# A hybrid decoder layer on one NeuronCore: other orders of the same steps on TensorE, ScalarE and VectorE

## What is computed

```
z  = rms_norm(h) @ w_in                         # 3328 columns: RWKV-7 inputs and q, k, v
h += concat(rwkv7_time_mix(z), moba(q, k, v)) @ w_mix_out
h += cross_attention(rms_norm(h), rms_norm(mem))  # 4 heads of 256: w_xq, w_xkv, w_xo
h += square(relu(rms_norm(h) @ w_ff1)) @ w_ff2    # 1024 -> 4096 -> 1024
out = rms_norm(h)
```

## Time and profile before

| | us |
|---|---|
| median of 3 runs | 488.88 |
| the profiled execution, its own time | 492.94 |
| its span in the trace | 491.0 |
| TensorE busy (matmuls) | 467.5 |
| VectorE busy | 331.4 |
| ScalarE busy | 238.4 |

### The profile page before, as it was taken

How to read it: one execution, slowest core, us unless ns; L and a number is a source line. 1 busy time by engine, 2 the same in 40 slices (tenths; PEclk the granted TensorE clock), 3 DMA queues, 4 the chain that set the end, 5 groups by cost and what they waited for, 6 DMA issues and landing times.

```text
span 491.0 us, 10602 instructions
## 1 busy us (share of the span) xinstructions
PE 467.5 (95%) x4518; PEld 422.9 (86%) x4518; DVE 331.4 (68%) x492; ACT 238.4 (49%) x384; POOL 35.6 (7%) x55
## 2 busy tenths in 40 slices
PE   4899999999899999989999999999999999999995
PEld 4899999989887889989999898887888888888883
DVE  3976998975156883946955569567656485756656
ACT  5788625245074433424644454555444443544444
POOL 8300000000000000015100024000000000000000
PEclk9997999999799999999999999999999999999999
DMA  7945254330233342255552236356575557466522
GB/s 251 298 160 174 87 172 131 118 101 10 81 110 90 121 137 87 87 172 171 167 178 85 87 94 206 130 166 192 167 246 156 195 166 238 159 245 191 157 82 85
DMA packets 61411, 73.07 MB, mean 149 GB/s; under 512 B 1315, under 2 KB 51573, under 8 KB 61365
## 3 DMA queue, kind: packets, MB, share of 16 engines
q1 hardware_dynamic: 61284, 72.14, 45.8%
q0 software_dynamic: 80, 0.26, 0.2%
HBM read 71.35 MB, written 1.05 MB: 147 GB/s over the span
## 4 chain that ended last, share of the span: by engine, by line
PE 74%; DVE 15%; ACT 4%; issue 3%; DMA 1%; SPq 1%; DVEq 0%; ACTq 0%
PE bank L522 8%; PE bank L536 8%; PE bank L538 8%; PE bank L537 8%; PE bank L554 6%; PE bank L556 6%; PE bank L555 6%; DVE w_lo L1271 5%; PE bank L520 5%; PE bank L744 2%; PE bank L489 2%; ACT w_hi L971 2%; PE bank L491 2%; PE bank L490 2%; PE bank L897 1%
## 5 line engine op out<-in xcount | busy, mean ns | idle before, releaser
L1271 DVE TENSOR_TENSOR w_lo<-raw,w_hi 128x1024 fp32r<-128x1024 f32 x130 | 159.9, 1240 | 66.9 <-ACT w_hi L971 66.6
L971 ACT ACTIVATE w_hi<-raw 128x1024 fp32r<-128x1024 f32 x130 | 136.0, 1056 | 107.1 <-PE bank L538 51.5
L536 PE MATMUL bank<-op,w_hi 128*128 128x256 f32 x416 | 123.0, 296 | 4.1 <-DVE w_lo L1271 2.3
L537 PE MATMUL bank<-op,w_hi 128*128 128x256 f32 x416 | 118.4, 285 | 0.0
L538 PE MATMUL bank<-op,w_lo 128*128 128x256 f32 x416 | 118.3, 284 | 0.0
L536 PEld LDWEIGHTS bank<-op,w_hi 128*128 128x128 f32 x416 | 80.5, 194 | 7.3 <-issue 4.8
L537 PEld LDWEIGHTS bank<-op,w_hi 128*128 128x128 f32 x416 | 80.6, 194 | 0.2
L538 PEld LDWEIGHTS bank<-op,w_lo 128*128 128x128 f32 x416 | 80.4, 193 | 0.0
L522 PE MATMUL bank<-op,w_hi 128*128 128x512 f32 x224 | 80.0, 396 | 0.0
L520 PE MATMUL bank<-op,w_lo 128*128 128x256 f32 x256 | 66.4, 280 | 0.1
L520 PEld LDWEIGHTS bank<-op,w_lo 128*128 128x128 f32 x256 | 48.3, 189 | 2.9 <-DVE op L1352 0.4
(11 more groups left out here) (254 smaller groups left out, 612.1 us busy)
## 6 DMA issues: line engine op xcount, KB each, us to landing
raw<-in_w_ff SPq DMA_DIRECT2D x32, 1024.0 KB, 5.4
raw<-in_w_in SPq DMA_DIRECT2D x12, 1024.0 KB, 5.3
raw<-in_w_xkv SPq DMA_DIRECT2D x8, 1024.0 KB, 5.5
raw<-in_w_mix_out SPq DMA_DIRECT2D x4, 1024.0 KB, 5.2
raw<-in_w_xq SPq DMA_DIRECT2D x4, 1024.0 KB, 5.1
raw<-in_w_xo SPq DMA_DIRECT2D x4, 1024.0 KB, 5.2
xval<-in_x SPq DMA_DIRECT2D x2, 512.0 KB, 4.8
raw<-in_w_in SPq DMA_DIRECT2D x2, 512.0 KB, 5.8
```

Source lines behind the costliest of these rows:

```text
L536: mm(dst, wh[:, k, :], op_hi[which][:, k, :], start=first, stop=False)
L537: mm(dst, wh[:, k, :], op_lo[which][:, k, :], start=False, stop=False)
L971: op(view(w_hi), r, ACT.Copy).then_inc(hi_done, 1)
L1271: tt(view(w_lo), r, view(w_hi).bitcast(f32), ALU.subtract).then_inc(lo_done, 1)
```

## The change

Three lists of steps are replaced by others with the same steps; no step's own code changes, but for one wait added to `shifted` on VectorE (for `dve_bonus`). The lists of TensorE, ScalarE and VectorE in short, with "..." for parts that are left out:

```diff
 TensorE
-load(0, 0); params(0); load(0, 1); load(0, 2); load(0, 3); dense(2); params(1); dense(3); spread(0)
-dense(3); lora(); dense(8); key_sums(); dense(1); key_spread(); dense(8); spread(1); dense(6)
-load(1, 0); load(1, 1); tokens(); dense(1); bonus(); dense(1); values_turn(); dense(1); mats(0)
-load(1, 2); dense(2); load(1, 3); mats(1); dense(4); right(0); right(1); dense(3); right(2)
-right(3); dense(2); solve(0); solve(1); solve(2); pair_scores(0); solve(3); carry(0); carry(1)
-carry(2); carry(3); dense(2); solved(0); solved(1); solved(2); solved(3); dense(3); outq(0, 0)
-outq(0, 1); outq(0, 2); dense(1); pair_turn(0, 0); outq(0, 3); outq(1, 0); outq(1, 1); dense(1)
-pair_turn(0, 1); outq(1, 2); outq(1, 3); dense(1); pair_values(0); dense(1); phi(0); pair_scores(1)
-phi(1); dense(2); psi(0, 0); psi(0, 1); psi(0, 2); psi(0, 3); psi(1, 0); dense(1); psi(1, 1)
-psi(1, 2); psi(1, 3); dense(2); pair_turn(1, 0); pair_turn(1, 1); state(1); pair_values(1); dense(1)
-pair_scores(2); dense(2); state(2); dense(2); pair_turn(2, 0); pair_turn(2, 1); state(3)
-pair_values(2); dense(1); pair_scores(3); dense(1); state(4); dense(1); state(5); dense(1)
-pair_turn(3, 0); dense(1); pair_turn(3, 1); state(6); dense(1); states_out(); pair_values(3)
-dense(1); center(); dense(3); deviation(); dense(2); normalize(); gate(); dense(24); rms(2)
-dense(5); scores(0); dense(4); scores(1); turn(0); ...
+load(0, 0); params(0); load(0, 1); load(0, 2); load(0, 3); dense(2); params(1); dense(2); spread(0)
+dense(6); lora(); dense(6); key_sums(); dense(2); key_spread(); dense(8); spread(1); dense(6)
+load(1, 0); load(1, 1); tokens(); dense(2); bonus(); values_turn(); dense(2); mats(0); dense(2)
+mats(1); dense(2); right(0); right(1); load(1, 2); right(2); load(1, 3); dense(8); right(3)
+solve(0); solve(1); solve(2); carry(0); pair_scores(0); solve(3); carry(1); carry(2); solved(0)
+carry(3); solved(1); solved(2); solved(3); dense(2); pair_turn(0, 0); pair_turn(0, 1); outq(0, 0)
+outq(0, 1); outq(0, 2); outq(0, 3); dense(4); pair_values(0); outq(1, 0); outq(1, 1); outq(1, 2)
+outq(1, 3); dense(2); phi(0); pair_scores(1); phi(1); dense(5); psi(0, 0); psi(0, 1); psi(0, 2)
+psi(0, 3); psi(1, 0); psi(1, 1); psi(1, 2); psi(1, 3); dense(3); pair_turn(1, 0); pair_turn(1, 1)
+state(1); pair_values(1); dense(1); state(2); pair_scores(2); dense(4); pair_turn(2, 0)
+pair_turn(2, 1); state(3); pair_values(2); dense(1); pair_scores(3); state(4); dense(3); state(5)
+dense(1); state(6); dense(2); states_out(); dense(1); center(); dense(2); deviation(); dense(1)
+pair_turn(3, 0); normalize(); pair_turn(3, 1); pair_values(3); gate(); dense(21); rms(2); dense(5)
+scores(0); dense(3); scores(1); turn(0); ...
 ScalarE
-...; stats(0); split(); split(); split(); split()
-follow(0); gates(); split(); follow(1); rates(); split(); stats(1); split(); follow(2); key_sums()
-split(); split(); follow(3); key_norm(); decays(); ...
-... solve(0); solve(1); solve(2); carry(0); solve(3); pair_exp(0, 0); carry(1)
-carry(2); carry(3); pair_exp(0, 1); split(); split(); split(); pair_turn(0, 0); out_take(0) ...
+...; stats(0); split(); split(); split(); follow(0)
+gates(); split(); split(); split(); follow(1); rates(); split(); follow(2); key_sums(); split()
+stats(1); key_norm(); follow(3); split(); split(); decays(); ...
+... right(3); solve(0); carry(0); solve(1); solve(2); solve(3)
+carry(1); pair_exp(0, 0); pair_exp(0, 1); carry(2); carry(3); pair_turn(0, 0); pair_turn(0, 1) ...
 VectorE
-params(0); load(0, 0); load(0, 1); load(0, 2); copies(0); load(0, 3); diagonal_of(0); split()
-params(1); copies(1); spread_copy(0); take(0); split(); split(); follow(0); split(); take(1)
-split(); follow(1); sums(); take(2); split(); follow(2); split(); take(3); split(); key_floor() ...
-... split(); bonus(); load(1, 0)
-split(); split(); load(1, 1); take(7); masked(0); mats(0); mats(1); take(8); invert(0) ...
-... split(); shifted(); state(1); ...
-... deviation(); split(); pair_values(3); split(); normalize(); gate(0); gate(1); split(); gate_low(0) ...
+params(0); load(0, 0); load(0, 1); load(0, 2); load(0, 3); diagonal_of(0); params(1); split()
+split(); spread_copy(0); take(0); split(); follow(0); copies(0); copies(1); take(1); split()
+follow(1); split(); split(); take(2); follow(2); split(); sums(); take(3); split(); key_floor() ...
+... bonus(); shifted(); take(7); split(); masked(0); load(1, 0); load(1, 1); take(8); mats(0); mats(1) ...
+... invert(4); split(); take(10); load(1, 2); invert(5); load(1, 3); ...
+... deviation(); split(); normalize(); pair_values(3); take(19); gate(0); gate(1); gate_low(0) ...
             def shifted():
+                dve.wait_ge(dve_bonus, 1)
                 for p in range(NP):
```

More of the change, by code:

```diff
@@ L938, in _ @@
+            values(1); dense(1); turn(2); scores(3); dense(1); values(2); turn(3); dense(1); values(3)
             dense(14)
@@ L1230, in _ @@
[L1230 to L1243, removed]
+            load(0, 0); load(0, 1); load(0, 2); load(0, 3); stats(0); split(); split(); split(); follow(0)
@@ new lines, in _ @@
+            gates(); split(); split(); split(); follow(1); rates(); split(); follow(2); key_sums(); split()
+            stats(1); key_norm(); follow(3); split(); split(); decays(); follow(4); split(); keys(2); split()
+            split(); follow(5); split(); split(); tokens(); split(); follow(6); load(1, 0); split(); load(1, 1)
+            split(); bonus(); split(); split(); right(0); split(); split(); split(); right(1); load(1, 2)
+            right(2); load(1, 3); split(); split(); right(3); solve(0); carry(0); solve(1); solve(2); solve(3)
@@ new lines, in _ @@
+            carry(1); pair_exp(0, 0); pair_exp(0, 1); carry(2); carry(3); pair_turn(0, 0); pair_turn(0, 1)
+            split(); split(); out_take(0); out_take(1); split(); out_take(2); out_take(3); pair_values(0)
+            split(); pair_exp(1, 0); phi_take(); split(); pair_exp(1, 1); split(); psi_take(0); psi_take(1)
+            psi_take(2); psi_take(3); split(); pair_turn(1, 0); pair_turn(1, 1); split(); pair_values(1)
+            pair_exp(2, 0); split(); pair_exp(2, 1); split(); pair_turn(2, 0); pair_turn(2, 1); pair_values(2)
@@ new lines, in _ @@
+            split(); split(); pair_exp(3, 0); pair_exp(3, 1); split(); split(); deviation(); split()
+            head_root(); split(); pair_turn(3, 0); pair_turn(3, 1); pair_values(3); gate(0); gate(1); split()
+            split(); split(); split(); split(); split(); split(); operand('mix', 0); split(); operand('mix', 1)
+            operand('mix', 2); split(); operand('mix', 3); split(); rms(2); split(); split(); split(); scores(0)
+            split(); turn(0); values(0); scores(1); split(); split(); turn(1); scores(2); split(); values(1)
@@ L1244, in _ @@
+            split(); turn(2); scores(3); values(2); turn(3); values(3); split(); split(); split(); split()
+            follow(29); follow(30); split(); split(); follow(31); split()
             at[0] = PHASE["xo"]
@@ new lines, in _ @@
+            spread_copy(1); reads(); take(6); split(); weighted(); tokens(); follow(6); split(); split()
+            bonus(); shifted(); take(7); split(); masked(0); load(1, 0); load(1, 1); take(8); mats(0); mats(1)
+            invert(0); masked(1); invert(1); split(); invert(2); split(); take(9); invert(3); split(); split()
+            invert(4); split(); take(10); load(1, 2); invert(5); load(1, 3); split(); pair_mask(0, 0); take(11)
+            pair_mask(0, 1); pair_share(0, 0); solved(0); split(); solved(1); pair_share(0, 1); solved(2)
@@ new lines, in _ @@
+            pair_mask(3, 1); scale(4); state(4); split(); scale(5); state(5); pair_share(3, 0); pair_share(3, 1)
+            take(17); scale(6); state(6); split(); split(); take(18); states_out(); split(); center(0)
+            center(1); split(); deviation(); split(); normalize(); pair_values(3); take(19); gate(0); gate(1)
+            gate_low(0); gate_low(1); split(); split(); take(20); take(21); split(); split(); take(22); split()
+            split(); split(); operand('mix', 0); take(23); operand('mix', 1); operand('mix', 2); split()
@@ L1732, in _ @@
+            operand('mix', 3); split(); take(24); rms(2); split(); take(25); split(); split(); split()
+            scores(0); take(26); weigh(0); scores(1); split(); values(0); weigh(1); take(27); split(); split()
+            scores(2); weigh(2); values(1); take(28); split(); scores(3); split(); weigh(3); values(2)
+            values(3); split(); split(); take(29); split(); follow(29); split(); take(30); split(); take(31)
+            follow(30); split(); follow(31); split(); take(32)
             at[0] = PHASE["xo"]
```

37 lines of the change are left out of this document (9 added, 28 removed).

## The result

The changed kernel takes **485.08 us** (median of 4 runs, 484.62 to 485.80) beside 488.64 us for the kernel before (4 runs, 488.31 to 489.62): a ratio of 0.9925, 95% interval 0.9905 to 0.9946, or 3.6 us. It is faster, as forecast, and inside the range, but the forecast gain was 8.9 us. The profiled execution took 484.73 us (span 482.9), against 492.94 before.

The account below looks back on a forecast made before the run. TensorE bounds the kernel. Gains of 12.1 us (waits 4.7, clock 5.6, runs 1.8), less new waits 2.1 and hand-overs 1.1, leave 8.9: from the 488.9 us median to 480.0, range 476.5 to 486.5.

Parts of the forecast that it names:

- The inverses ready at 103.3: 50 to 104 us: VectorE finishes the inverses at 103.3, about 0.5 us after `right(3)`, with TensorE's lead kept.
- around `normalize`: 140 to 210 us: new TensorE waits of 0.8 us for `deviation` and 0.3 for `pair_values(3)`, 1.1 us against.
- The pause "issue" that I kept in the sum: TensorE's 1.35 us stop inside `outq(0, 2)`, laid to used-up instructions; assumed to stay, so nothing gained.
- Rival (c): VectorE bounds 50 to 104 us and the lead is lost at the inverses: 5 us less, 485.0; chance 0.1.
- its median stands 4.1 us lower, and I take the difference off the median: Whole kernel: the 8.9 us gain, found on the profiled execution, is subtracted from the 488.9 us median, giving 480.0.
- two stretches at half clock: At 42.5 to 49.2 and 127.8 to 134.6 us: both go, gaining 2.8 us each, 5.6 together.
- rival (b): Unprofiled runs have no stretch at half clock, so the gain is only 3.3 us, 485.6; chance 0.17.
- From 210 us. The same quarters and small steps ... Nothing, with 0.5 us either way: From 210 us on: same work, `turn(1)`'s thin cover hidden by two quarters; no gain, 0.5 us either way.
- 9 x 0.2 = 1.8 us: TensorE's runs of small steps fall from 50 to 41, each costing some 0.2 us: 1.8 us gained.
- the thin places: 50 to 104 us: five places with waits under 1 us or under 0.5 to spare, set against two earlier waits.
- the hand-overs: Each hand-over costs 0.1 to 0.2 us beyond the walk, counted at some eight thin places: 1.1 us against.
- Rival (a): The clock falls again once, around `outq` or after `key_sums`: 2.8 us less gained, 482.8; chance 0.23.

Follow-up runs that it names:

- first experiment: The kernel before, word for word, profiled and timed again: 489.86 us over 12 runs, ratio 0.9992 to the runs of before beside it.
- e0: The kernel before, unchanged, profiled a second time: 489.86 us (12 runs), profiled execution 490.42 us.
- e3_both: The changed kernel with ScalarE's and VectorE's last list lines as before, and one VectorE split moved ahead of two operand steps: 479.72 us, ratio 0.9787.
- e6: The kernel before with only ScalarE's `stats(1)` moved behind the key squares and VectorE's `sums` behind `take(2)` and `follow(2)`: 493.86 us, ratio 1.0086.
- e7: `e3_both` with `outq(0, *)` and `psi` broken up by single quarters at 8 more places: 485.36 us, ratio 0.9906.
- e8: `e3_both` with `outq(0, *)` alone broken up by three single quarters: 482.48 us, ratio 0.9852.
- e1: The changed kernel with the last part of ScalarE's and VectorE's lists, behind `values(3)`, as in the kernel before: 482.75 us, ratio 0.9846.
- e5: The changed kernel with ScalarE's `stats(1)` put back ahead of `follow(2)` and the key squares: 490.93 us, ratio 1.0024.
- e2: The changed kernel with one VectorE split moved ahead of `operand('mix', 1)` and `operand('mix', 2)`: 483.29 us, ratio 0.9855.
- e10: `e3_both` with `pair_turn(3, 1)` and `pair_values(3)` ahead of `normalize`, and `take(19)` behind `gate(0)`: 481.88 us, ratio 0.9841.

## Why the prediction was right or wrong

**Right: what bounds, and the walk to 210 us.** TensorE is the bound, 95% busy before and after. "The inverses ready at 103.3" stands against 102.07, and a first `solve` "within 1 us of 103.5" against 102.13, 1.4 us early and so 0.4 outside, on the good side; no idle time ahead of `key_sums`; `key_spread` late by 0.20 (0.4 forecast); around `normalize` 0.27 + 0.58 + 0.33 = 1.2 us of idle time (1.1 forecast, though as 0.8 and 0.3, so the sum is nearer than its parts); the wait of 1.76 us at the 82nd quarter gone. The pause "issue" that I kept in the sum is there, 0.96 us instead of 1.35, but not in `outq`: it is in a dense quarter behind `psi`, at 147.07. Rival (c), VectorE as the bound of the inverses, did not come, but by little: the inverses end 0.06 us before `solve` starts.

**Wrong, first step: "its median stands 4.1 us lower, and I take the difference off the median".** The sum had 5.6 us from two stretches at half clock of one execution, 13.6 us together. The second profile of the same kernel has 6.8, and all 57 further runs had a higher mean clock than the one I read. Against the median the clock was worth between a gain of 0.7 us and a loss of about 1 us, depending on which runs of before one takes (first experiment). That is rival (b) in its cause, to which I gave 0.17: the other explanation, that the profiler itself costs the 4.1 us, is spoken against by the second profiled execution, whose 490.42 us lie among its other runs' 487.93 to 490.99. This step has **4.9 us** of the miss (5.6 less 0.7) by `e0`'s clocks, and up to 6.6 by the runs beside the result. The new stretch behind the wait at 296 is contained in it.

**Wrong, second step: "From 210 us. The same quarters and small steps ... Nothing, with 0.5 us either way".** I looked only at TensorE's list and at `values(0)`, and took the rest of VectorE's and ScalarE's lists as not mattering, though the sections not shown had splits and takes at other places. Two waits of 1.86 and 3.05 us came, where the second had a smaller forerunner before, and a stretch at half clock. Two small edits of these lists are worth some **5 us** (479.72 against 485.08 us, spans 478.0 against 482.9): 3.7 us are the waits themselves, and the rest is mostly clock, which the first step has already.

**Mis-sized: "9 x 0.2 = 1.8 us", the thin places and the hand-overs.** A run costs 0.37 us, so nine are 3.3, **1.5 us** more gained. From 50 to 104 us I set two waits of before against what the thin places would cost; of the two, 0.55 and 0.6 us, only 0.26 came back, **0.9 us** more. And the 1.1 us for hand-overs at eight thin places have no wait in the profile that would carry them. So 8.9 - 4.9 - 3.7 + 1.5 + 0.9 + 1.1 = 3.8 us with 4.9 for the clock, and 2.1 with 6.6; measured were 3.6. Which of the two holds can't be said, as the clock of those four runs isn't known.

Between the second profile of before and the one of after this question doesn't arise. The span goes from 488.5 to 482.9, 5.6 us. TensorE's idle times, added up over its whole timeline, go from 16.9 to 15.8 us (1.1), the half clock from two stretches of 3.4 us to one of 3.4 (1.2), and nine runs at 0.37 are 3.3: 5.6 together. At the 82nd quarter the lead is 9.2 us: the idle times up to there go from 14.1 to 8.9 us (5.2), one stretch at half clock is 1.2, the runs 3.3, together 9.7. That the price of a run, measured at `outq`, holds at all nine places is assumed in these sums, not shown.

**Rival (a).** It said that the clock falls again once and named `outq` or `key_sums`. It fell once in the profile of after, but behind the wait at 296, for which I had no case; and it cost about 1.1 us (3.3 x 0.34) instead of 2.8. Behind the pause at 147.07 it did not fall. `outq` as the place came from the pause and from the rule that transposes do not count as busy for the clock (the Trainium skill, page "TensorE: Matmul & The Clock Gate", section "Part 4: PE-mode transpose"). The trace doesn't bear it out here: the clock row of after is 9 from the first slice to 290 us, with the transposes of `pair_turn(0, *)` at 117.30 and `outq` behind them in it.

**How the errors lie to one another.** Against the profile that it read, the forecast was close: 484.0 for 484.73. That is luck: the lead at the 82nd quarter was 13.2 us, not about 9, and 5 us were lost behind it. On the medians the errors do not cancel, and 3.6 us are left of 8.9. With the second error mended (`e3_both`) the kernel takes 479.72 us. This is where the forecast stood, again by terms that offset: less from the clock, more from the runs and thin places. The clock can be set aside by comparing the runs with a mean clock of 0.998 or more: median 488.45 us for the kernel before (15 runs, 487.93 to 489.36), 479.66 for `e3` (4 runs, 479.44 to 479.96). The new orders with these two edits save 8.8 us at equal clock; the idle times, 16.9 us in `e0` and 12.6 in `e3`, and nine runs make 7.6 of it.

**The pauses called "issue".** The prediction had it that TensorE runs out of instructions in `outq`. The times of the instruction packets (queue q8 of the earlier trace rows) bear that out. In the 13 profiles TensorE has 28 pauses of 0.25 us or more that are called "issue" and are not the wait ahead of `key_sums`. Every one ends 1.2 to 1.6 us after such a packet has landed: 126.06 after 124.73 in the profile before, 123.57 after 122.33 in `e0`, 147.07 after 145.68 in the one after. Packets begin some 4.6 us apart here (median from 100 to 155 us), so this is hardly chance. A packet mostly takes 1.1 us; ahead of the three pauses in `outq(0, 2)`, 1.35 (before), 1.05 (`e6`) and 0.80 us (`e0`), it took 2.65, 2.25 and 2.02. So where the pause falls depends on how fast TensorE uses its instructions and on how long their transfer takes: behind `psi` after the change (147.07), gone from there when `psi` is broken up (`e7`), in `outq(1, 2)` and behind `psi` in `e8`. No run moved the code without moving the steps, so this is read from the traces and not tested.

**Open.** Why the same wait is followed by a low clock in some executions and not in others.

## What to carry to other kernels

Look at the clock of several executions before pricing it: a stretch at half clock belongs to one execution, and if the profiled run is not near the median, take the forecast against that run apart into waits, which stay, and clock, which may not. When an order is rewritten, walk every engine's list to its last line, also where TensorE's own list is unchanged; a split behind work that shares its time with POOL is where the gain went here. And try moves in the company that they need: one step gave some 5 us in the new lists, and nearly the same move cost 3.9 in the old.

## What was not expected of the hardware

- The mean granted clock of one and the same kernel varies from 0.987 to 0.999 between 11 runs on one core, and the time follows it, 0.34 us for each microsecond at half clock on one chip and less on two others. In the 13 profiles every stretch at half clock, but for the ends of the span, came within an idle time of TensorE or at most 3 us behind it: 0.85 us (and again in `e0`), 0.77 (`e8`), 1.35, 1.72 (`e7`), 1.77 (`e0`), 1.86 (`e1`, `e5`), 2.79 (`e5`), 3.04 to 3.05 (after, `e2`, `e5`), 4.24 (`e6`, already within it). The 1.86 us in the profile of after, the 1.76 of the earlier trace rows, 1.93 (`e10`) and all the pauses of 0.64 to 0.97 us behind `psi` were followed by none, while 1.77 us at the place of the earlier trace rows in `e0` was.
- VectorE and POOL slow one another: 3.44 us against 1.68 for the same four instructions, and 5 to 6 us of the kernel's time, the clock behind the waits included, until the order gave VectorE slack.
- Changing between dense and small fp32 steps costs TensorE 0.37 us a run, measured at three breaks in `outq`, with no idle record at all, so it is invisible in the waits and shows only as the distance between steps.
- TensorE can run out of instructions in dense quarters as well as in small matmuls: all 28 pauses without a releaser end 1.2 to 1.6 us after an instruction packet has landed.
